# Router on the raw rows: norm weights folded into the router, rows normalised by ScalarE and GpSimd, last jobs in another order

## The reference

```python
h = rms_norm(x, norm_mix_g);  proj = h @ w_in          # conv group | attention group (8 heads of 64)
...
x = x + concat(conv_out, attn_out) @ w_out
h2 = rms_norm(x, norm_ffn_g)                           # y / rms(y) * g, y is this new x
x = x + hierarchical_moe(h2, w_router_group, w_router_expert, ...)

def hierarchical_moe(h, w_rg, w_re, w_g, w_u, w_d):
    lg = h @ w_rg                                      # 4 groups, the largest is taken
    le = h @ w_re                                      # 8 experts in the group, two are taken
    ...                                                # rows sorted by expert, blocks of 128, SwiGLU experts
```

## Time and profile before

| | us |
|---|---|
| median of 3 runs | 2188.38 (2186.2 to 2188.7) |
| span of the profiled execution | 2187.6 |
| TensorE busy | 2089.9 (96%) |
| VectorE busy | 1616.3 (74%) |
| ScalarE busy | 1259.0 (58%) |
| GpSimd busy | 767.6 (35%) |

### The profile page before, as it was taken

The page is one execution under the profiler, slowest core; times in us unless marked ns, Lnnn a source line. Parts: engine busy times, 40 slices in busy tenths (PEclk is TensorE's granted clock), DMA queues, the critical chain, the costliest instruction groups (busy, mean ns, idle before and its releaser), DMA issues. The chain is left out here.

```text
span 2187.6 us, 40169 instructions
## 1 busy us (share of the span) xinstructions
PE 2089.9 (96%) x13511; PEld 1763.6 (81%) x13512; DVE 1616.3 (74%) x2084; ACT 1259.0 (58%) x2199; POOL 767.6 (35%) x696
## 2 busy tenths in 40 slices
PE   8999999996899999899999897999999999999998
PEld 6888888885687887678787775888888888888887
DVE  3799999994777667867878868879699556466644
ACT  5322433344677677866676644768678456455533
POOL 1111444553566565645545453211111112111111
PEclk9999999996999999999999998999999999999999
DMA  7563334434333233433222116989899968667851
GB/s 227 190 205 136 120 126 155 133 107 144 108 123 110 80 111 102 115 100 116 80 73 93 54 71 247 377 309 370 299 369 373 305 205 279 216 208 264 286 165 35
DMA packets 211805, 393.17 MB, mean 180 GB/s; under 512 B 54781, under 2 KB 81789, under 8 KB 211677
## 3 DMA queue, kind: packets, MB, share of 16 engines
q1 hardware_dynamic: 198141, 357.42, 47.1%
q0 software_dynamic: 13536, 34.12, 6.6%
HBM read 315.42 MB, written 91.23 MB: 186 GB/s over the span
## 5 line engine op out<-in xcount | busy, mean ns | idle before, releaser
L2528 DVE TENSOR_TENSOR p_w_lo<-p_raw,p_w_hi 128x1024 fp32r<-128x1024 f32 (+1 forms) x196 | 330.3, 1718 | 134.2 <-ACT p_w_hi L2320 133.6
L2124 POOL TENSOR_TENSOR late<-late,p_past 128x1024 f32<-128x1024 f32 (+4 forms) x166 | 308.2, 1857 | 341.9 <-DVE p_past L1981 338.7
L796 DVE SCALAR_TENSOR_TENSOR p_ut<-p_ut,p_cw 128x512 f32<-128x512 f32 (+1 forms) x480 | 329.2, 760 | 0.0
L2320 ACT ACTIVATE p_w_hi<-p_raw 128x2048 fp32r<-128x2048 f32 (+1 forms) x150 | 271.6, 1842 | 62.1 <-PE p_up L2412 53.3
L1981 DVE TENSOR_TENSOR_SCAN p_past<-p_keep,p_past,p_one 128x513 f32<-128x513 f32 (+1 forms) x196 | 225.9, 1192 | 76.6 <-ACT p_keep L1798 74.6
L1798 ACT ACTIVATE p_keep<-p_zp 128x512 f32<-128x512 f32 (+3 forms) x326 | 158.8, 547 | 114.3 <-PE p_zp L1672 101.6
L2412 PE MATMUL p_gp<-p_w_hi,p_xt_hi 128*128 128x256 f32 x736 | 214.3, 291 | 0.0
L473 PE MATMUL p_pj<-p_w_hi,p_xt_hi 128*128 128x512 f32 x512 | 205.2, 401 | 4.2 <-DVE p_xt_lo L772 2.4
L2412 PE MATMUL p_gp<-p_w_lo,p_xt_hi 128*128 128x256 f32 x736 | 206.4, 280 | 0.0
L2412 PE MATMUL p_gp<-p_w_hi,p_xt_lo 128*128 128x256 f32 x736 | 206.4, 280 | 0.0
L473 PE MATMUL p_pj<-p_w_hi,p_xt_lo 128*128 128x512 f32 x512 | 200.6, 392 | 0.0
(11 more groups left out here) (315 smaller groups left out, 5005.2 us busy)
## 6 DMA issues: line engine op xcount, KB each, us to landing
p_raw<-in_w_up SPq DMA_DIRECT2D x96, 512.0 KB
p_raw<-in_w_gate SPq DMA_DIRECT2D x96, 512.0 KB
p_raw<-in_w_down SPq DMA_DIRECT2D x96, 512.0 KB
late<-in_w_up SPq DMA_DIRECT2D x32, 512.0 KB
late<-in_w_gate SPq DMA_DIRECT2D x32, 512.0 KB
late<-in_w_down SPq DMA_DIRECT2D x32, 512.0 KB
wide_raw<-in_w_in SPq DMA_DIRECT2D x56, 256.0 KB, 4.0
wide_raw<-in_x SPq DMA_DIRECT2D x17, 512.0 KB
```

Source lines behind the costliest of these rows:

```text
L796: dve.scalar_tensor_tensor(dst, src, cw[:, a, j:j + 1], dst, ALU.mult, ALU.add).then_inc(tap_done, 1)
L2124: pool.tensor_tensor(mine, mine, past_rows[:, u % NP, 0:n, 2:2 + w], ALU.mult).then_inc(a_done, 1)
L2320: act.activation(part(w_hi, p, wide), ring(n, wide), ACT.Copy).then_inc(whi_done, wide)
L2528: dve.tensor_tensor(part(w_lo, p, wide), ring(n, wide), part(w_hi, p, wide).bitcast(F32), ALU.subtract).then_inc(wlo_done, wide)
```

## The change

The router's product reads the transposed raw `y`. The weights of the norm are multiplied into the router's weights once (`router_gain`, GpSimd), and the logits are multiplied by `rstd` of their row as VectorE copies them out of PSUM. The normalised rows are still stored: ScalarE multiplies `y` by `rstd` (`scale_rows`), GpSimd multiplies by `g2` (`hidden`), both some steps later. `rstd` becomes a ring of six. The planner's table of costs, the steps of the stores and of the y loads, the hand-written list of last jobs and the placing of the one-hot tiles change too. Loads of y now also wait for TensorE's transposes of the tile three before.

```diff
@@ attention_jobs
-                then = s + 5 if s < end or job[1] == 2 * NT - 1 else s + 2
+                then = s + 2
                 later(("h2t", job[1], 0), then, then + 2)
@@ tail (hand-written, from step end on)
-    tail = [[], [], [("wo", z - 1, 0)], [("h2t", z - 2, 0), ("h2t", z - 2, 1)], [("o", z)],
+    tail = [[("route", z - 2)], [], [("wo", z - 1, 0)], [], [("o", z)],
...
@@ steps
-        hidden_step = [{m: e + (3 + c if e < end else 1 if m < 2 * NT - 1 else 2)
-                        for m, e in end_step.items() if m >= NT} for c in range(2)]
-        square_step = {m: e + 1 if e < end else e for m, e in end_step.items() if m >= NT}
+        square_step = {m: e + 1 if e < end or m == 2 * NT - 1 else e for m, e in end_step.items() if m >= NT}
+        scale_step = {m: s + (3 if s < end else 1) for m, s in square_step.items()}
+        hidden_step = {m: e + (5 if e < end else 2) for m, e in end_step.items() if m >= NT}
+        store_step = {m: e + (7 if e < end else 5) for m, e in end_step.items() if m >= NT}
...
-            y_step[m] = max(y_step[m], end_step[m - 3] + (5 if m - 3 >= NT else 1))
+            y_step[m] = max(y_step[m], end_step[m - 3] + (7 if m - 3 >= NT else 1))
...
-            act += 10 * sum(1 for m, e in end_step.items() if m >= NT and e == s - 1)
-            dve += 10 * sum(1 for half in hidden_step for e in half.values() if e == s)
+            act += 10 * sum(1 for m, e in square_step.items() if e == s) + 10 * sum(1 for e in scale_step.values() if e == s)
@@ load_y
-                    sp.wait_ge(h2_done, 2 * (m - 3 - NT) + 2)
+                    sp.wait_ge(h2_done, m - 3 - NT + 1)
+                    sp.wait_ge(mp_full, use["h2t", m - 3, 1] + 1)
@@ TensorE
-                    pe.wait_ge(h2_done, 2 * r + c + 1)
+                    pe.wait_ge(y_done, 2 * j[1] + c + 1)
                     for k in range(4):
                         last = pe.transpose(bank[:, k * P:(k + 1) * P],
-                                            h2[:, r % 2, (4 * c + k) * P:(4 * c + k + 1) * P], ident[:, :])
+                                            y[:, j[1] % 3, (4 * c + k) * P:(4 * c + k + 1) * P], ident[:, :])
@@ ScalarE
+            def scale_rows(m):
+                r = m - NT
+                act.wait_ge(rs_step, 2 * r + 2)
+                act.activation(h2[:, r % 2, :], y[:, m % 3, :], ACT.Copy, scale=rstd[r % RR]).then_inc(scaled, 1)
@@ VectorE
-                    dve.tensor_copy(lg[:, x, :], bank[:, 0:NG]).then_inc(lg_done, 1)
-                    dve.tensor_copy(le[:, x, :], bank[:, NG:NR]).then_inc(lg_done, 1)
+                    dve.wait_ge(rs_step, 2 * (j[1] - NT) + 2)
+                    scale = rstd[(j[1] - NT) % RR]
+                    dve.tensor_scalar(lg[:, x, :], bank[:, 0:NG], scale, None, ALU.mult).then_inc(lg_done, 1)
+                    dve.tensor_scalar(le[:, x, :], bank[:, NG:NR], scale, None, ALU.mult).then_inc(lg_done, 1)
...
-            def hidden(m, c):
-                r, mine = m - NT, slice(c * C, (c + 1) * C)
-                dve.wait_ge(const_in, 48)
-                dve.wait_ge(rs_step, 2 * r + 2)
-                dve.scalar_tensor_tensor(h2[:, r % 2, mine], y[:, m % 3, mine], rstd, g2[:, mine], ALU.mult,
-                                         ALU.mult).then_inc(h2_done, 1)
@@ GpSimd
+            def router_gain():
+                pool.wait_ge(const_in, 64)
+                pool.tensor_tensor(wr[:, :, :], wr[:, :, :], g2_col[:, :].unsqueeze(2).broadcast_to([P, KT, NR]),
+                                   ALU.mult).then_inc(wr_done, 1)
+
+            def hidden(m):
+                r = m - NT
+                pool.wait_ge(scaled, r + 1)
+                pool.tensor_tensor(h2[:, r % 2, :], h2[:, r % 2, :], g2[:, :], ALU.mult).then_inc(h2_done, 1)
...
-            home_step = {end + 5: (0, 3), end + 6: (3, 5), end + 7: (5, 13), end + 9: (13, 2 * EARLY)}
+            home_step = {end + 5: (0, 3), end + 6: (3, 7), end + 7: (7, 13), end + 9: (13, 2 * EARLY)}
...
+                for m in at_step(hidden_step, s):
+                    if s < end + 5 or m == 2 * NT - 1:
+                        hidden(m)
...
+                if s == end + 7:
+                    hidden(2 * NT - 2)
```

More of the change, by code:

```diff
@@ L1211, in attention_jobs @@
     z = 2 * NT - 1
-    tail = [[], [], [("wo", z - 1, 0)], [("h2t", z - 2, 0), ("h2t", z - 2, 1)], [("o", z)],
-            [("wo", z - 1, 1), ("mix", z), ("route", z - 2)], [("wo", z, 0), ("h2t", z - 1, 0), ("h2t", z - 1, 1)],
-            [("wo", z, 1)], [("route", z - 1)], [("h2t", z, 0), ("h2t", z, 1), ("rank", len(BATCHES) - 2)],
-            [("route", z)], [], [], [("rank", len(BATCHES) - 1)]]
+    tail = [[("route", z - 2)], [], [("wo", z - 1, 0)], [], [("o", z)],
+            [("wo", z - 1, 1), ("mix", z), ("h2t", z - 1, 0), ("h2t", z - 1, 1)],
+            [("wo", z, 0), ("route", z - 1), ("rank", len(BATCHES) - 2)], [("wo", z, 1), ("h2t", z, 0)],
+            [("h2t", z, 1)], [("route", z)], [], [], [("rank", len(BATCHES) - 1)]]
     assert sorted(j for x in tail for j in x) == sorted(j for s in placed if s >= end for j in placed[s])
@@ L1241, in phase_attend @@
         NW, NK, NP, NA, NZ = 4, 2, 3, 4, 2
+        RR = 6
         HW = MAXU * P
@@ L1277, in phase_attend @@
         go = sb("go", [P, CT])
-        st = sb("st", [P, 16])
+        st = sb("st", [P, 15 + RR])
         oms, orr, ort = st[:, 0:4], st[:, 4:8], st[:, 8:12]
-        ss, rt, rstd = st[:, 12:13], st[:, 13:14], st[:, 14:15]
+        ss, rt, rstd = st[:, 12:13], st[:, 13:14], [st[:, 14 + n:15 + n] for n in range(RR)]
         mhalf = sb("mhalf", [P, 4])
@@ L1522, in _ @@
                     sp.dma_start(dst[t * P:(t + 1) * P, :], y[:, m % 3, :]).then_inc(st_y[m % 3], 16)
-                for m in at_step(end_step, s - 5):
-                    if m >= NT:
-                        t, r = tile_of(m), m - NT
-                        sp.wait_ge(h2_done, 2 * r + 2)
-                        sp.dma_start(scr["h2"][t * P:(t + 1) * P, :], h2[:, r % 2, :]).then_inc(st_h[r % 2], 16)
+                for m in at_step(store_step, s):
+                    t, r = tile_of(m), m - NT
+                    sp.wait_ge(h2_done, r + 1)
+                    sp.dma_start(scr["h2"][t * P:(t + 1) * P, :], h2[:, r % 2, :]).then_inc(st_h[r % 2], 16)
                 for g, kt in at_step(k_step, s):
@@ L1630, in job @@
                     r = j[1] - NT
-                    pe.wait_ge(const_in, 48)
+                    pe.wait_ge(wr_done, 1)
                     pe.wait_ge(h2t_done, 2 * r + 2)
@@ L1834, in squares @@
                     act.wait_ge(st_h[r % 2], 16 * (r // 2))
-                    act.wait_ge(mp_full, use["h2t", m - 2, 1] + 1)
                 act.activation(h2[:, r % 2, :], y[:, m % 3, :], ACT.Square, accum_out=ss).then_inc(ss_done, 1)
+            def scale_rows(m):
+                r = m - NT
+                act.wait_ge(rs_step, 2 * r + 2)
+                act.activation(h2[:, r % 2, :], y[:, m % 3, :], ACT.Copy, scale=rstd[r % RR]).then_inc(scaled, 1)
             for j in jobs[-1]:
@@ L1858, in _ @@
                     squares(m)
+                for m in at_step(scale_step, s):
+                    scale_rows(m)
         @block.vector
@@ L2028, in _ @@
             for s in range(steps):
-                for c in (1, 0) if s < len(units) else (0, 1):
-                    for m in at_step(hidden_step[c], s):
-                        hidden(m, c)
                 for n in at_step(piece_step, s - 1):
@@ L2112, in inverse_rms @@
                 if r:
-                    pool.wait_ge(h2_done, 2 * r)
+                    pool.wait_ge(rs_step, 2 * r)
+                if r >= RR:
+                    pool.wait_ge(lg_done, 2 * (r - RR + 1))
+                    pool.wait_ge(h2_done, r - RR + 1)
                 pool.tensor_scalar(rt, ss, 1.0 / D, EPS, ALU.mult, ALU.add).then_inc(rs_step, 1)
                 pool.wait_ge(rs_step, 2 * r + 1)
-                pool.tensor_tensor(rstd, rt, mhalf[:, 0:1], ALU.pow).then_inc(rs_step, 1)
+                pool.tensor_tensor(rstd[r % RR], rt, mhalf[:, 0:1], ALU.pow).then_inc(rs_step, 1)
+            def router_gain():
[6 more added lines that the diff above has]
+                pool.tensor_tensor(h2[:, r % 2, :], h2[:, r % 2, :], g2[:, :], ALU.mult).then_inc(h2_done, 1)
             def product(u):
@@ L2147, in _ @@
                     rank_constants()
+                if s == first[NT] // 2 + 4:
+                    router_gain()
                 for m in at_step(split_step, s):
@@ L2681 @@
         "norm_ffn_g": a["norm_ffn_g"][0],
+        "norm_ffn_col": cols(a["norm_ffn_g"][0], KT),
         "w_out": a["w_out"][0],
```

8 lines of the change are left out of this document (5 added, 3 removed).

## The result

The changed kernel takes 2203.11 us (median, 2199.12 to 2204.14), against 2188.32 of the kernel before in the same runs: ratio 1.0061, 95% interval [1.0049, 1.0073]. By the ratio it is 13.4 us slower (the two medians are 14.8 us apart), where 3.9 us faster was forecast. The span of its profile is 2202.2 us.

The account below looks back on a forecast made before the run. TensorE, busy 331.5 of 350 us, was nearly full in attention's second half, its longest waits for VectorE; the tail a chain of waits. -12.3 + 1.0 + 0 + 5.4 + 2.0 = -3.9 against 2187.6: forecast 2184, range 2174 to 2191.

Parts of the forecast that it names:

- VectorE loses `hidden`: Second half of attention: 34 instructions leave VectorE's queue, shortening TensorE's waits and slow clock; -12.3 us.
- I take 1 us of small delays; the ends are 0 and 4: ScalarE's 17 scalings and GpSimd's 17 products fit in those engines' free time; +1.0 us, ends 0 and 4.
- rival 2: GpSimd's products stop VectorE's choice of experts where TensorE waits, taking 7 us back; 2188 to 2191 us, chance 0.13.
- its sign: For rival 2: L1906 or L1881's likes exceed 1.5 us more often, and TensorE's waits at 1222 us remain.
- Route scales on the way out: Router logits: two copies per tile become two multiplies from the same bank; 0 us, ends -1 and +1.
- The tile y: Near 978 us: y of tile 20 loads behind loads of v, so VectorE's add and TensorE wait; +5.4 us.
- The tail: From 1290 us: GpSimd's queue delays mix 33 and the last homes; +2.0 us, ends -4 and +5.
- Rival 1: The late tile and GpSimd's tail are absorbed, mix 33 waits no longer than before; 2177 us, chance 0.20.
- Rival 3: y comes late at every tight place, tiles 21 to 27; 12 us more, 2196; with other losses, chance 0.12.

Follow-up runs that it names:

- b2_no_hidden: Kernel before with VectorE's `hidden` left out, nothing in its place; ratio 0.9901, not to be read since expert choice changes; attention phase -13.9 us in its trace.
- c2_c1_no_product: c1_y20_and_order with GpSimd's product by the norm's weights left out; ratio to the kernel before 0.9956.
- c1_y20_and_order: Changed kernel with the earlier load of y for tile 20 and the old order for h2t, last jobs and homes put back; ratio to before 1.0010.
- e1_y20_early: Changed kernel with the load of y for tile 20 one step earlier in SP's queue, ahead of two loads of v; ratio to before 1.0033.
- f3_tail_on_vector: f1_product_beside_none with `hidden` of tiles 31 to 33 done by VectorE; 2179.5 us, ratio to before 0.9966.
- f1_product_beside_none: c1_y20_and_order with three GpSimd products that ran beside choice or ranks (tiles 22, 23, 29) put two steps later; ratio to before 0.9993.
- f2_new_h2t_only: c1_y20_and_order with only the new h2t rule (two steps behind wo, not five), last jobs and homes as before; ratio to before 1.0027.

## Why the prediction was wrong, step by step

The forecast's terms, and what the traces gave when they were taken apart one by one (from b2_no_hidden over c2_c1_no_product, c1_y20_and_order and e1_y20_early to the changed kernel; each is the difference of two traces, of one execution each, between 933 us and the end of the phase):

| term | forecast | measured |
|---|---|---|
| VectorE loses `hidden` | -12.3 | -13.9 |
| ScalarE's scaling, `rstd`'s ring, route's scaling | +1.0 with the next | +2.8 |
| GpSimd's product | (in the line above) | +14.4 |
| h2t's rule and the last jobs | +2.0 | +4.2 |
| tile 20 late | +5.4 | +6.8 |
| sum | -3.9 | +14.4 |

By the ratios the product is 11.8 us, the order 5.0, the tile 6.1. The rows of the forecast do not match those measured everywhere: its +2.0 is for the tail with GpSimd's products in it, of which 4.2 us stand in the product's row here, and it had h2t's rule in the body only as 1.3 us of waits inside its first term.

*VectorE loses hidden: right.* The trace without it gives 13.9 us. In the body it is 10.9, a little under the 12.3; the other three come in the tail, for which the term had none, so the nearness of the sum is in part luck.

*"I take 1 us of small delays; the ends are 0 and 4": this is the step that failed.* In place of 1 us the product alone cost 11.8 us by the ratios and 14.4 in the traces. The forecast priced 17 products by whether anything waits for GpSimd, and in the body of the changed kernel TensorE never does; only mix 33, in the tail, waits for GpSimd, 4.5 us. The price was on the other engine: a product beside the choice or the ranks holds a VectorE instruction of 0.17 to 0.3 us for up to 2.35 us, and these stand ahead of an add, a copy or a split for which TensorE waits. The forecast saw this (L1881 at 1.53 us beside GpSimd, 0.17 alone), worked it out as rival 2 and gave it 0.13 and 7 us, with the argument that product and choice meet in few tiles. That is so: in the body they meet in three of fourteen. But in c1_y20_and_order these three cost 3.7 us by the ratios and 6.9 in the traces at 1260 us, and two more in the tail meet the choice or the ranks of the last two batches. Moving the tail's three to VectorE (f3_tail_on_vector against f1_product_beside_none) gave 5.9 us by the ratios, 4.7 in the traces. Some 3 us of the product's price in the body stay open.

The Trainium skill, "SBUF — State Buffer", on the shared port pair, gives the rule: a VectorE instruction with two inputs in SBUF and a GpSimd instruction that reads SBUF take turns, each for the whole instruction. The trace agrees, to 0.04 us at 1226. By that rule the stall is as long as what is left of GpSimd's instruction, not as long as VectorE's.

*Route scales on the way out:* its cost was not separated from the other 2.8 us. Its instructions take 0.21 and 0.24 us, where the copies took 0.15 and 0.18.

*The tile y: right in place and cause, too small in size.* 5.4 forecast, 6.1 to 6.8 measured; the wait was 5.4 at TensorE where 3.7 was said. The load was issued at 978.60, the add began 4.7 us later; the forecast took 977.21 and a landing of 2.9.

*The tail: the wait right, the end not.* The wait before mix 33 was 4.5 us (3 to 4 said); GpSimd's last home ended at 1335.86 us, 1.8 us before VectorE and 3.1 before the end of the phase (within 1 us was said). The end was not set by GpSimd but by the last choice, beside which `hidden` of 33 ran. The tail costs 4.5 us from 1288 us on, where 2.0 were said: mix 33 comes 2.9 us later than the body alone would make it, and 1.6 us are added behind it. The last route is no part of this: it took 3.49 us here and 3.60 before (the 1.87 of the earlier trace rows is the route of tile 32).

*What the forecast did not price:* the rule for h2t in the body, 3.7 us (f2_new_h2t_only). It was counted only as a wait of some 1.3 us. Taking h2t sooner makes the planner place k and q elsewhere, so that their splits on VectorE stand behind or between the parts of the choice; TensorE then waits for `kt` (L1935) and `q_lo` (L1940) at 1158 and 1236 us. The order is read from the traces; no run moved these jobs alone.

*Rivals.* Rival 1 fell in both its parts: neither the late tile nor the tail was absorbed, they cost 6.1 to 6.8 and 4.5 us. Rival 2 was the right mechanism with too low a price, 7 us; its sign came, as instructions of the choice and the ranks over 1.5 us went from four to seven. Rival 3's other tiles were never late: no other add waits for a DMA.
